# Three transformer blocks on one core: two groups of quarter products placed by a new timetable

## The chip, the cores and the metric

One core of a Trainium2 chip runs one program. The metric is device time in microseconds (us). The kernel before took 1427.65 us (median of three runs, 1426.95 to 1429.47).

## The reference

A sequence of 256 tokens of width 1024 in float32 goes through two blocks of one kind and one of another. The change concerns the first kind, and in it the two feed-forward parts:

```python
def rms_norm(x, g):
    y = xf * lax.rsqrt(jnp.mean(xf * xf, axis=-1, keepdims=True) + EPS)
    return (y * g.astype(jnp.float32)).astype(x.dtype)

def swiglu(h, w_gate_up, w_down):
    a, b = jnp.split(h @ w_gate_up, 2, axis=-1)       # 1024 -> 2 x 2816
    return (jax.nn.silu(a) * b) @ w_down              # 2816 -> 1024

def hybrid_layer(x, ...):
    x = x + 0.5 * swiglu(rms_norm(x, ffn1_norm), ffn1_w_gate_up, ffn1_w_down)
    ...                                               # pooling, attention, gates
    x = x + 0.5 * swiglu(rms_norm(x, ffn2_norm), ffn2_w_gate_up, ffn2_w_down)
    return x
```

`hybrid_layer` runs twice; a block of another kind follows, with its own feed-forward part.

## The kernel before

**Stages.** The program goes through eight stages: L0f1, L0 (mixer), L0f2, L1f1, L1, L1f2 (the four names with f are the *gated* feed-forward stages, `GATED`), then M and Mf. All 256 tokens stay in SBUF, the weights stream through.

**Precision and tiles.** A float32 product is made of three reduced ones. ACT copies each weight tile (128 x 1024, 512 KB) to a high part `whi` (line 1332), DVE subtracts to get the low part `wlo` (line 1936); such a pair of steps is called a split here. PE multiplies high by high, high by low and low by high. SP loads plain tiles into a ring of 8 buffers `raw` (line 597), waiting for the split that frees each. `whi` and `wlo` are rings of 6. ACT and DVE split some 5 and 4 tiles ahead (`ahead`).

**Gated stage.** Of the 22 blocks of 128 hidden features, two come first (group p). Twelve are *gate pairs* N2 to N10 and N15 to N17: tiles a and b, 16 matmuls of 128x512 (line 716) and 16 of 128x256 (line 723); both PSUM banks of a pair from N4 on are claimed before its first matmul. The other eight, blocks 11 to 14 and 18 to 21, are made as two *groups* (a and b in the table, chunk 0 and 1 in the code) by seven quarter products instead of eight: products 1 to 7, 12 matmuls each (lines 875 to 879). Products 3, 5, 6 and 7 use sums of the input's quarters, the input forms: DVE builds them in `xf`, ACT writes the high part `yhi` (line 1425), DVE the low part `ylo` (line 2034, `input_low`). *d i* adds block i to the output accumulators (lines 670 to 672), *T* turns a group's result for d11 and on.

**Weight forms.** Products 1 and 5 use buffer G, products 3, 7, 6 and 4 buffer H, in that order. SP loads the first form (line 615, `load_form`); each next one is made in place: when both halves of a product's tile have been split by DVE, POOL issues an accumulating DMA that adds another quarter of the weights (line 2645, `add_form`); ACT waits for it to land before it splits the next product. Group b's buffer H1 lies over `xf`, so its first load waits for the semaphore `xf_lo`, that of `input_low`. It stands in SP's queue after tile b6.

**Combining.** The products of a group are combined from PSUM by `chunk` on ACT (lines 1413 to 1421) and DVE (lines 2044 to 2060). These run when the engine comes to its next `catch_up`: after `whole(i, 0)` in a gate pair, or after the first `ahead` of a d or P step. DVE's step for product 6 releases 6's bank ("comb" + 1); ACT's SiLU of product 2 releases the bank in which 1 and 2 were summed ("sil").

**Order.** The string `ORDER` is the timetable of all five engines: PE runs it word by word, ACT and DVE do for each word their splits and what belongs to it, SP loads tiles in that order, POOL adds. `banks` hands out four PSUM banks in turn in the order of PE's claims and notes for each what frees it; banks of products 1 and 7 are held until 2 and 4 are done. So the table also sets which step each claim waits for. In the first group's last product POOL also makes tables for the next mixer (`prepare1`, `prepare2`).

```python
                        if i > 3:
                            ba, bb = claim((tag, "a", i)), claim((tag, "b", i))
                            high_part(ja, ba)
...
                    if kind == "P":
                        ahead(T[f"{tag}s{i}{n}0"])
                        catch_up()
                        ahead(T[f"{tag}s{i}{n}1"])
                        due.append((i, n))
```

Of the kernel before, what the change touches and what calls it, by code (L numbers as in the profile page):

```python
# [110 lines left out]
for _t in [f"L{l}g{j}{f}" for l in range(2) for f in range(KD) for j in range(2) if f or j]:  # L111
    HI_LEAD[_t], LO_LEAD[_t] = 4, 3
GATED = ("L0f1", "L0f2", "L1f1", "L1f2")
ORDER = """N2 N3 d0 1a N4 d1 2a N5 d2 3a N6 d3 7a N7 d4 6a N8 d5 5a N9 d6 4a N10 d7 3b d8 T0a 1b d9 T1a 7b d10 2b d11 6b
           N15 d12 5b N16 d13 4b N17 d14 d15 T0b d16 T1b d17""".split()
GROUPS = (11, 18)
CHUNK = {o + q: (c, q) for c, o in enumerate(GROUPS) for q in range(4)}
# [8 lines left out]
def steps():  # L126

    for n, word in enumerate(ORDER):
        if word[0] in "Nd":
# [7 lines left out]
def turned_hidden():  # L137

    at, out = {word: n for n, word in enumerate(ORDER)}, {}
    for i, (c, q) in CHUNK.items():  # L140
# [276 lines left out]
def build_program(nc, x_in, wstream, gains, const_in, par_in, out, cat, pat, plan, addends):  # L417
# [3 lines left out]
    with ExitStack() as ctx:  # L421
# [886 lines left out]
        def act_program(E):  # L1308
# [41 lines left out]
            def norm_hi(n, a, part=(0, 1)):  # L1350
                for g in part:
                    E.wait_ge("xt", 4 * n + 2 * a + g + 1)
                    if n:
                        E.wait_ge("tile", K.last_up(n - 1))
                    b = bank[K.BANK["xt", n, a, g][0]]
                    e.activation(feat(0, g, a), by4(b[:, :]), ACT.Copy).then_inc(sem["xhi"], 2 if n == a == 0 else 1)
# [28 lines left out]
            def gated(s):  # L1385
                tag = STAGES[s]
                f = FFNS.index(tag)
                norm_hi(s, 1)
                hi_upto(T[f"{tag}p0"] + 5)
                halves = lambda t: t.rearrange("p (n j f) -> p n j f", j=2, f=P)  # L1390
                for a in range(2):
                    E.wait_ge("tok", K.TOK[f"{tag}p"]) if a == 0 else E.wait_ge("tile", K.TOKTILE[f"{tag}p"])
                    b = bank[K.BANK[f"{tag}p", a][0]]
                    tb = tokbuf[:, a * 512:a * 512 + 512]
                    e.activation(v3d(tb[:, 0:S], 2, P), halves(b[:, :])[:, :, 0, :], ACT.Silu).then_inc(sem["tok_a"], 1)

                def low(i, part):

                    E.wait_ge("tile", DONE[f"{tag}{'ab'[part]}{i}"])
                    m = K.MUL0[s] + NORMAL.index(i)  # L1400
                    if m >= 2:
                        E.wait_ge(*(K.PROD_FREE if part else K.SIL_FREE)[m - 2])
                    e.activation((prod if part else sil)[m % 2][:, :], bank[K.BANK[tag, "ab"[part], i][0]][:, S:2 * S], ACT.Copy).then_inc(sem["low"], 1)

                def chunk(c, n):

                    cc = K.chunk_no(tag, c)
                    if n in (1, 2, 3):
                        E.wait_ge("tile", DONE[f"{tag}s{c}{n}1"])
                        b = bank[K.BANK[tag, "s", c, {2: 1}.get(n, n)][0]]  # L1410
                    if n == 1:
                        E.wait_ge("tokm", 3 * cc)
                        e.activation(tokU, b[:, :], ACT.Copy).then_inc(sem["tokp"], 1)
                    if n == 2:
                        E.wait_ge("turn", 2 * cc)
                        e.activation(tokS, b[:, :], ACT.Silu).then_inc(sem["sil"], 1)
                    if n == 3:
                        e.activation(tokV, b[:, :], ACT.Copy).then_inc(sem["tokv"], 1)
                    if n == 4:
                        E.wait_ge("comb", 5 * cc + 5)  # L1420
                        e.activation(tokU, tokU, ACT.Silu).then_inc(sem["sil"], 1)

                def input_forms():
                    E.wait_ge("xf", 6 * GATED.index(tag) + 6)
                    e.activation(yhi[:, :], xf, ACT.Copy).then_inc(sem["xf_hi"], 1)

                def turned(i):
                    c, q = CHUNK[i]
                    E.wait_ge("turn", 2 * K.chunk_no(tag, c) + q // 2 + 1)
                    if q % 2:  # L1430
                        E.wait_ge("hidlo", K.HID0[s] + i)
                    hidden_hi(K.HID0[s] + i, bank[K.BANK[tag, "turn", c, q // 2][0]][:, q % 2 * S:q % 2 * S + S])

                due = []

                def catch_up():
                    while due:
                        chunk(*due.pop(0))

                for at, kind, i, n in steps():  # L1440
                    if kind == "N":
                        ja, jb = T[f"{tag}a{i}"], T[f"{tag}b{i}"]
                        ahead(ja)
                        if i == 2:
                            E.wait_ge("ft", K.FT[tag, 0])
                            t = bank[K.BANK[tag, "ft", 0][0]]
                            for n in range(2):
                                if n:
                                    E.wait_ge("hidlo", K.HID0[s] + 1)
                                hidden_hi(K.HID0[s] + n, t[:, n * S:n * S + S])  # L1450
                        low(i, 0)
                        catch_up()
                        ahead(jb)
                        m = K.MUL0[s] + NORMAL.index(i)
                        sl = sil[m % 2][:, :]
                        E.wait_ge("sum", K.SUMV[s, i] + 1)
                        e.activation(sl, sl, ACT.Silu).then_inc(sem["act"], 1)
                        low(i, 1)
                        if i == 3:
                            input_forms()  # L1460
                        E.wait_ge("mul", K.MULV[s, i])
                        hidden_hi(K.HID0[s] + i, prod[m % 2][:, :])
                    if kind == "d":
                        ahead(T[f"{tag}d{i}"])
# [6 lines that stand above are left out]
                    for h_ in TURNED.get(at, ()):  # L1471
                        catch_up()
                        if h_ == NF - 1:
                            hi_upto(T[f"{tag}d{h_}"])
                        turned(h_)
                finish(s)
# [450 lines left out]
        def dve_program(E):  # L1927
# [70 lines left out]
            def gated(s):  # L1998
# [69 lines left out]
                for at, kind, i, n in steps():  # L2068
                    if kind == "N":
                        ja, jb = T[f"{tag}a{i}"], T[f"{tag}b{i}"]  # L2070
                        ahead(ja)
                        if i == 2:
                            t = bank[K.BANK[tag, "ft", 0][0]]
                            for n in range(2):
                                hidden_lo(K.HID0[s] + n, t[:, n * S:n * S + S])
                        whole(i, 0)
                        catch_up()
                        ahead(jb)
                        whole(i, 1)
                        m = NORMAL.index(i)  # L2080
                        pr, sl = prod_of(s, m), sil[(K.MUL0[s] + m) % 2]
                        E.wait_ge("act", K.MULV[s, i])
                        E.wait_ge("sum", K.SUMV[s, i] + 2)
                        e.tensor_tensor(pr[:, :], sl[:, :], pr[:, :], ALU.mult).then_inc(sem["mul"], 1)  # L2084
                        hidden_lo(K.HID0[s] + i, pr[:, :])
                        if i == 2:
                            input_sum(0)
                            input_sum(1)
                            input_forms()
                        if i == 3:  # L2090
                            input_low()
                    if kind == "d":
                        ahead(T[f"{tag}d{i}"])
# [6 lines that stand above are left out]
                    for h_ in TURNED.get(at, ()):  # L2100
                        catch_up()
                        if h_ == NF - 1:
                            lo_upto(T[f"{tag}d{h_}"])
                        c, q = CHUNK[h_]
                        hidden_lo(K.HID0[s] + h_, bank[K.BANK[tag, "turn", c, q // 2][0]][:, q % 2 * S:q % 2 * S + S])
# [853 lines left out]
```

## Time and profile before

| | |
|---|---|
| median of three runs | 1427.65 us |
| the profiled execution | 1427.81 us |
| its span | 1426.0 us |
| PE matmul | busy 1414.3 us, 99% |
| DVE | busy 1063.6 us, 75% |
| ACT | busy 838.7 us, 59% |
| POOL | busy 200.9 us, 14% |
| DMA | 292.90 MB, mean 205 GB/s |
| TensorE clock | full in all 40 slices |

The profile is of one execution; its times count from the start of the span. An engine's waits are listed by what released it. A busy share says little here: PE is the engine that sets the time, and what others do matters where PE waits for it. Matmuls are pipelined: one of 128x512 is shown with 0.39 us, and the next starts 0.23 us after it.

### The profile page before, as it was taken

The numbers are of one execution on the slowest core, as the hardware profiler recorded it, in microseconds if no ns is written. First come the engines' busy times: TensorE is split into PE (matmuls) and PEld (weight loads), VectorE is DVE, ScalarE is ACT, GpSimd is POOL, SyncE is SP. The second block draws the span as 40 slices with busy tenths as digits, with TensorE's granted clock in tenths as the row PEclk, the third lists the DMA queues.
The fourth block names the chain that finished last, engine by engine and source line by source line (L and its number), as shares of the span: only waits on it lengthen the run. The fifth ranks groups of instructions, "written<-read, shape, count | busy, mean of one in ns | idle before, by whom it ended". The sixth has DMA issues, their size and how long they took to land.

```text
span 1426.0 us, 20401 instructions
## 1 busy us (share of the span) xinstructions
PE 1414.3 (99%) x7776; PEld 1207.5 (85%) x7776; DVE 1063.6 (75%) x1638; ACT 838.7 (59%) x1397; POOL 200.9 (14%) x275
## 2 busy tenths in 40 slices
PE   9999999999999999999999999999999999999999
PEld 7888888898888888888888898888888899888887
DVE  7777776676867778786776678777776867778776
ACT  6556556755665556664566746655557765455553
POOL 0121023000001000210050000141048300100000
PEclk9999999999999999999999999999999999999999
DMA  9979665456887768967564466969646335456551
GB/s 376 310 215 241 202 214 180 134 192 226 264 233 182 213 235 271 251 171 213 192 236 148 163 216 184 306 188 244 198 160 222 134 121 192 161 166 219 194 189 59
DMA packets 80592, 292.90 MB, mean 205 GB/s; under 512 B 8944, under 2 KB 9072, under 8 KB 80368
## 3 DMA queue, kind: packets, MB, share of 16 engines
q1 hardware_dynamic: 70992, 257.26, 51.5%
q0 software_dynamic: 9216, 33.56, 13.0%
q8 instruction: 62, 1.02, 0.3%
q10 hardware_dynamic: 288, 0.79, 0.1%
q14 instruction: 34, 0.28, 0.1%
HBM read 290.52 MB, written 1.05 MB: 204 GB/s over the span
## 4 chain that ended last, share of the span: by engine, by line
PE 92%; DVE 5%; ACT 1%; DMA 1%; issue 0%; SPq 0%; DVEq 0%; ACTq 0%
PE bank L716 19%; PE bank L723 10%; PE bank L670 8%; PE bank L671 8%; PE bank L672 8%; PE bank L737 4%; PE bank L742 4%; PE bank L738 4%; PE bank L875 3%; PE bank L879 3%; PE bank L876 3%; PE bank L700 3%; PE bank L707 3%; PE bank L701 3%; DVE wlo L1936 2%; PE bank L969 1%
## 5 line engine op out<-in xcount | busy, mean ns | idle before, releaser
L1936 DVE TENSOR_TENSOR wlo<-raw,whi 128x1024 fp32r<-128x1024 f32 (+1 forms) x433 | 523.4, 1235 | 12.7 <-ACT whi L1332 12.7
L1332 ACT ACTIVATE whi<-raw 128x1024 fp32r<-128x1024 f32 (+1 forms) x433 | 443.0, 1049 | 6.0 <-DMA raw<-w_dram 2.9
L716 PE MATMUL bank<-hx,whi 128*128 128x512 f32 x1344 | 330.8, 393 | 2.1 <-issue 2.1
L716 PEld LDWEIGHTS bank<-hx,whi 128*128 128x128 f32 x1344 | 247.6, 188 | 54.7 <-issue 6.3
L670 PE MATMUL bank<-whi,hid 128*128 128x512 f32 x536 | 211.8, 395 | 0.0
L671 PE MATMUL bank<-wlo,hid 128*128 128x512 f32 x536 | 209.6, 391 | 0.0
L672 PE MATMUL bank<-whi,hid 128*128 128x512 f32 x536 | 208.8, 390 | 0.0
L723 PEld LDWEIGHTS bank<-hx,wlo 128*128 128x128 f32 x1344 | 176.0, 191 | 13.4 <-DVE wlo L1936 4.5
L723 PE MATMUL bank<-hx,wlo 128*128 128x256 f32 x1344 | 179.5, 283 | 3.7 <-DVE wlo L1936 3.7
L1361 ACT ACTIVATE hid<-prod 128x256 fp32r<-128x256 f32 x94 | 39.3, 418 | 161.0 <-DVE prod L2084 75.9
L672 PEld LDWEIGHTS bank<-whi,hid 128*128 128x128 f32 x536 | 100.6, 188 | 21.7
L670 PEld LDWEIGHTS bank<-whi,hid 128*128 128x128 f32 x536 | 101.0, 188 | 18.8 <-issue 0.7
L671 PEld LDWEIGHTS bank<-wlo,hid 128*128 128x128 f32 x536 | 101.0, 188 | 17.2
L737 PE MATMUL bank<-whi,hx 128*128 128x512 f32 (+1 forms) x256 | 101.9, 399 | 1.2 <-DVE hx L1964 0.9
L738 PE MATMUL bank<-whi,hx 128*128 128x512 f32 (+1 forms) x256 | 98.1, 384 | 0.0
L742 PE MATMUL bank<-wlo,hx 128*128 128x512 f32 (+1 forms) x256 | 77.5, 385 | 0.0
L1969 DVE TENSOR_TENSOR hid<-prod,hid 128x256 fp32r<-128x256 f32 x94 | 40.0, 426 | 47.0 <-ACT hid L1361 47.0
L2600 POOL TENSOR_SCALAR small<-small 128x1 f32<-128x1 f32 x15 | 10.7, 713 | 451.4 <-ACT arena L1347 451.4
L1936 DVE TENSOR_TENSOR wlo<-gates,whi 128x1024 fp32r<-128x1024 f32 x48 | 57.6, 1225 | 20.7 <-ACT whi L1332 20.7
L1936 DVE TENSOR_TENSOR wlo<-arena,whi 128x1024 fp32r<-128x1024 f32 x48 | 57.2, 1219 | 12.5 <-ACT whi L1332 12.5
L1332 ACT ACTIVATE whi<-arena 128x1024 fp32r<-128x1024 f32 x48 | 48.9, 1050 | 29.0 <-DMA arena<-w_dram 29.0
L1332 ACT ACTIVATE whi<-gates 128x1024 fp32r<-128x1024 f32 x48 | 49.4, 1053 | 26.0 <-DMA gates<-w_dram 26.0
(300 smaller groups left out, 2188.2 us busy)
## 6 DMA issues: line engine op xcount, KB each, us to landing
raw<-w_dram SPq DMA_DIRECT2D x438, 512.0 KB, 4.4
gates<-w_dram POOLq DMA_DIRECT2D x32, 512.0 KB, 6.7
arena<-w_dram POOLq DMA_DIRECT2D x32, 512.0 KB, 7.6
gates<-w_dram SPq DMA_DIRECT2D x16, 512.0 KB, 6.6
arena<-w_dram SPq DMA_DIRECT2D x16, 512.0 KB, 6.5
gain<-g_dram SPq DMA_DIRECT2D x7, 512.0 KB, 3.4
arena<-c_dram SPq DMA_DIRECT2D x2, 768.0 KB, 6.4
cst<-c_dram SPq DMA_DIRECT2D x1, 1056.0 KB, 10.2
```

The source lines that it names most:

```text
L670: e.matmul(psum, shi, mhi, start=first, stop=False, skip_group_check=True)
L671: e.matmul(psum, shi, mlo, start=False, stop=False, skip_group_check=True)
L672: return e.matmul(psum, slo, mhi, start=False, stop=last, skip_group_check=True)
L700: e.matmul(psum, whj[:, w:w + P], hi(k), start=k == 0, stop=False, skip_group_check=True)
L701: e.matmul(psum, whj[:, w:w + P], lo(k), start=False, stop=False, skip_group_check=True)
L716: e.matmul(b[:, :], hi_of(j)[:, k * P:k * P + P], hx[:, k * 2 * S:k * 2 * S + 2 * S], start=k == 0, stop=False, skip_group_check=True)
L723: ins = e.matmul(b[:, 0:S], lo_of(j)[:, k * P:k * P + P], hiT(k), start=False, stop=k == KD - 1, skip_group_check=True)
L737: e.matmul(b[:, 0:n], hiT(k, a * P, a * P + P), w, start=k == 0, stop=False, skip_group_check=True)
L738: e.matmul(b[:, 0:n], loT(k, a * P, a * P + P), w, start=False, stop=False, skip_group_check=True)
L742: ins = e.matmul(b[:, 0:n], hiT(k, a * P, a * P + P), w, start=False, stop=k == KD - 1, skip_group_check=True)
L1332: e.activation(hi_of(t), raw_of(t), ACT.Copy).then_inc(sem["w_hi"], 1)
L1936: e.tensor_tensor(lo_of(t), raw_of(t), hi_of(t).bitcast(F32), ALU.subtract).then_inc(sem["w_lo"], 1)
```

## The change

The low part of the input forms is made on DVE after gate pair N4 instead of N3. The timetable has another order from d4 on up to N15: product 5a before N8, then the rest of group a and products 3b, 1b, 7b and 2b each earlier against the gate pairs; d10 and d11 stand next to each other before 6b. ACT's copy of product 3 waits in the second group for the first multiply of the group before.

```diff
-ORDER = """N2 N3 d0 1a N4 d1 2a N5 d2 3a N6 d3 7a N7 d4 6a N8 d5 5a N9 d6 4a N10 d7 3b d8 T0a 1b d9 T1a 7b d10 2b d11 6b
+ORDER = """N2 N3 d0 1a N4 d1 2a N5 d2 3a N6 d3 7a N7 d4 6a 5a N8 d5 4a N9 d6 3b N10 d7 1b d8 T0a 7b d9 T1a 2b d10 d11 6b
            N15 d12 5b N16 d13 4b N17 d14 d15 T0b d16 T1b d17""".split()
...
                     if n == 3:
+                        if cc:
+                            E.wait_ge("tokm", 3 * cc - 2)
                         e.activation(tokV, b[:, :], ACT.Copy).then_inc(sem["tokv"], 1)
...
-                        if i == 3:
+                        if i == 4:
                             input_low()
```

In the order of the changed program the lines from 1418 on have numbers larger by 2.

**DVE, gate pairs N3 and N4 of stage L0f1.** hid3 belongs to N3, hid0 to N4; `wlo` from `raw` are splits of plain tiles. Before:

```order
L1969 TENSOR_TENSOR hid3<-prod1,hid3 128x256 [waits s_hidhi]
L2034 TENSOR_TENSOR ylo<-arena,yhi 128x2048 [waits s_xf_hi]
L1936 TENSOR_TENSOR wlo<-raw,whi 128x1024 [waits s_w_hi] x4
L2014 TENSOR_TENSOR sil0<-sil0,bank0 128x256 [waits s_low]
L1936 TENSOR_TENSOR wlo<-raw,whi 128x1024 [waits s_w_hi]
L2014 TENSOR_TENSOR prod0<-prod0,bank1 128x256 [waits s_low]
```

Now:

```order
L1971 TENSOR_TENSOR hid3<-prod1,hid3 128x256 [waits s_hidhi]
L1938 TENSOR_TENSOR wlo<-raw,whi 128x1024 [waits s_w_hi] x4
L2016 TENSOR_TENSOR sil0<-sil0,bank0 128x256 [waits s_low]
L1938 TENSOR_TENSOR wlo<-raw,whi 128x1024 [waits s_w_hi]
L2016 TENSOR_TENSOR prod0<-prod0,bank1 128x256 [waits s_low]
L2086 TENSOR_TENSOR prod0<-sil0,prod0 128x256 [waits s_sum,s_act,s_hidlo]
L1971 TENSOR_TENSOR hid0<-prod0,hid0 128x256 [waits s_hidhi]
L2036 TENSOR_TENSOR ylo<-arena,yhi 128x2048 [waits s_xf_hi]
```

`ylo` moved behind four splits, one more, and N4's own steps.

**SP, from the second group's first load of G on, stage L0f1** (the same in both programs): the first two `arena` rows are form G of group b, the row that waits for `xf_lo` is form H of group b.

```order
L615 DMA arena<-w_dram 128x1024 [waits s_sq_v,s_sq]
L615 DMA arena<-w_dram 128x1024
L597 DMA raw<-w_dram 128x1024 [waits s_w_lo]
L615 DMA arena<-w_dram 128x1024 [waits s_xf_lo]
L615 DMA arena<-w_dram 128x1024
L597 DMA raw<-w_dram 128x1024 [waits s_w_lo] x2
L622 DMA cst<-c_dram 128x2112
```

Nothing moved here; what moved is the DVE step that `xf_lo` stands for.

**DVE, from the end of N7 to N8, stage L0f1.** hid3 is N7's; `wlo` from `gates` are splits of form tiles; line 2044 (2046 now) is the step for product 6. Before:

```order
L1969 TENSOR_TENSOR hid3<-prod1,hid3 128x256 [waits s_hidhi]
L1936 TENSOR_TENSOR wlo<-raw,whi 128x1024 [waits s_w_hi] x2
L1936 TENSOR_TENSOR wlo<-gates,whi 128x1024 [waits s_w_hi] x2
L2014 TENSOR_TENSOR sil0<-sil0,bank1 128x256 [waits s_low]
L2044 TENSOR_TENSOR arena<-arena,bank2 128x512 [waits s_tokp,s_tile]
```

Now:

```order
L1971 TENSOR_TENSOR hid3<-prod1,hid3 128x256 [waits s_hidhi]
L1938 TENSOR_TENSOR wlo<-gates,whi 128x1024 [waits s_w_hi]
L1938 TENSOR_TENSOR wlo<-raw,whi 128x1024 [waits s_w_hi] x3
L2046 TENSOR_TENSOR arena<-arena,bank2 128x512 [waits s_tokp,s_tile]
L1938 TENSOR_TENSOR wlo<-gates,whi 128x1024 [waits s_w_hi] x2
```

The step for product 6 comes before N8's `whole` now, and behind four splits as before. On **PE**, product 5a (lines 875 to 879) began behind d5 (lines 670 to 672), a gate pair after 6a:

```order
L671 MATMUL bank7<-wlo,hid1 128x512
L672 MATMUL bank7<-whi,hid1 128x512
L875 MATMUL bank2<-whi,yhi 128x512 [waits s_w_hi,s_comb]
L876 MATMUL bank2<-whi,ylo 128x512
L875 MATMUL bank2<-whi,yhi 128x512
```

Now 5a stands in front of N8 (line 716):

```order
L879 MATMUL bank1<-wlo,yhi 128x512 [waits s_w_lo]
L879 MATMUL bank1<-wlo,yhi 128x512
L716 MATMUL bank3<-hx,whi 128x512 [waits s_w_hi,s_comb,s_sum]
L716 MATMUL bank3<-hx,whi 128x512 x7
L716 MATMUL bank2<-hx,whi 128x512 [waits s_w_hi]
```

The wait for "comb", the release of product 6's bank, was 5a's and is N8's now.

## Rows read from the trace of the kernel before

**Rows 1.** Waits of PE, the whole span: us in total, times, longest us.

```profile
PE bank L723 <- DVE wlo L1936: 3.7, 4, 0.9
PE bank L716 <- issue: 2.1, 3, 1.0
```

**Rows 2.** Timeline of PE, N4 and d1 of L0f1: start, length.

```profile
43.15 1.11 PE L723 MATMUL bank<-hx,wlo 128*128 128x256 f32 x8
45.17 1.22 PE L723 MATMUL bank<-hx,wlo 128*128 128x256 f32 x8 [0.91 <-DVE wlo L1936]
46.40 0.47 PE L670 MATMUL bank<-whi,hid 128*128 128x512 f32 x1
```

**Rows 3.** Chain that ended last: N8 of three stages, N15 of L1f1.

```profile
85.10 3.63 PE bank L716 x16
88.72 1.91 PE bank L723 x16
...
417.48 3.63 PE bank L716 x16
...
655.11 1.05 issue
656.15 3.88 PE bank L716 x16
...
933.08 3.63 PE bank L716 x16
```

**Rows 4.** Timeline of DVE, N3's end to product 3a's splits, L0f1.

```profile
41.70 2.29 DVE L2034 TENSOR_TENSOR ylo<-arena,yhi 128x2048 fp32r<-128x2048 f32 x1
43.90 4.63 DVE L1936 TENSOR_TENSOR wlo<-raw,whi 128x1024 fp32r<-128x1024 f32 x4
...
51.37 0.43 DVE L1969 TENSOR_TENSOR hid<-prod,hid 128x256 fp32r<-128x256 f32 x1 [0.48 <-ACT hid L1361]
...
53.98 2.35 DVE L1936 TENSOR_TENSOR wlo<-gates,whi 128x1024 fp32r<-128x1024 f32 x2
```

**Rows 5.** Timeline of ACT before N15, stage L1f1.

```profile
651.40 1.06 ACT L1332 ACTIVATE whi<-arena 128x1024 fp32r<-128x1024 f32 x1 [3.86 <-DMA arena<-w_dram]
...
655.47 0.58 ACT L1416 ACTIVATE arena<-bank 128x512 f32<-128x512 f32 x1
```

**Rows 6.** Timeline of SP's queue, L0f1: form H of group b, next tiles.

```profile
45.52 0.91 SPq L615 DMA_DIRECT2D arena<-w_dram  x2
46.47 1.27 SPq L597 DMA_DIRECT2D raw<-w_dram  x2
```

**Rows 7.** DMA rate in 40 slices of 1.5 us from 15 to 75 us.

```profile
GB/s 412 410 404 415 410 404 407 412 412 404 412 412 391 243 134 16 44 150 249 423 415 421 268 355 377 442 420 415 412 345 270 270 284 270 284 410 421 380 259 262
```

**Rows 8.** Timeline of ACT, L0f1: split of 6a's second tile, low of N7.

```profile
80.43 1.06 ACT L1332 ACTIVATE whi<-gates 128x1024 fp32r<-128x1024 f32 x1 [2.81 <-DMA gates<-w_dram]
...
82.34 0.36 ACT L1403 ACTIVATE sil<-bank 128x256 f32<-128x256 f32 x1
```

**Rows 9.** Timeline of DVE, L0f1: splits behind N7, step for product 6.

```profile
86.08 2.54 DVE L1936 TENSOR_TENSOR wlo<-raw,whi 128x1024 fp32r<-128x1024 f32 x2
...
90.93 0.41 DVE L2014 TENSOR_TENSOR sil<-sil,bank 128x256 f32<-128x256 f32 x1
91.26 0.67 DVE L2044 TENSOR_TENSOR arena<-arena,bank 128x512 f32<-128x512 f32 x1
```

**Rows 10.** The same splits of ACT in L0f2 and L1f2.

```profile
407.35 1.07 ACT L1332 ACTIVATE whi<-gates 128x1024 fp32r<-128x1024 f32 x1 [0.26 <-DMA gates<-w_dram]
...
411.09 0.38 ACT L1403 ACTIVATE sil<-bank 128x256 f32<-128x256 f32 x1 [1.73 <-PE bank L723]
...
924.31 1.07 ACT L1332 ACTIVATE whi<-gates 128x1024 fp32r<-128x1024 f32 x1 [0.40 <-DMA gates<-w_dram]
```

**Rows 11.** Timeline of DVE, L0f2: splits behind N7.

```profile
414.84 2.35 DVE L1936 TENSOR_TENSOR wlo<-raw,whi 128x1024 fp32r<-128x1024 f32 x2
```

**Rows 12.** Timeline of DVE, L1f1: the split in N7.

```profile
593.62 3.17 DVE L1936 TENSOR_TENSOR wlo<-raw,whi 128x1024 fp32r<-128x1024 f32 x1
```

## What the change does to the time, predicted

> **What bounds the kernel now.** I read the page first: TensorE is busy for 1414.3 of 1426.0 us, so only its waits can be won or added. The waits by engine [rows 1] name two kinds inside the four gated feed-forward stages: four waits for a `wlo` piece of DVE (3.7 us) and three put down to "issue" (2.1 us).
>
> *Wait A*, once in each stage, is in [rows 2]. The low part of N4's second tile (line 723) starts 2.02 us after the first instead of 0.96 (half of the 1.91 that the chain shows for N8 in [rows 3]); the next step starts 1.23 us later instead of 0.96; with a slow first matmul of 0.07 that is 1.4 us. [Rows 4] show why on DVE: the low part of the input forms (`ylo`, 2.29 us) runs at 41.70, ahead of four `wlo` splits that only begin at 43.90; the first is what PE waits for at 45.17, the second holds d1.
>
> *Wait B* is at N15, and only in the three later stages. In stage L1f1 the chain [rows 3] shows 1.05 us of "issue" before it, and a group of 16 that takes 3.88 us where N8's takes 3.63. On ACT [rows 5] a split waited 3.86 us for the added form of product 6b to land, and the SiLU of product 2b (line 1416), whose bank N15 claims, came behind it and ended at 656.05, just before PE starts at 656.15. Three such waits: 2.1 us of [rows 1], and some 0.3 each of slow restart, 3.0 in all.
>
> **The sum, part by part.** The profiled execution took 1427.81 us for a span of 1426.0; the median shown is 1427.65, 0.16 less. To set stages side by side I subtract 332.38 and 847.98 us from times of L0f2 and L1f2: the differences of their N8 starts to 85.10 [rows 3].
>
> 1. *`input_low` one gate pair later.* The four `wlo` splits run at about 41.7 to 46.4, the two that PE wants ending near 42.9 and 44.1 instead of 45.1 and 46.3 (1.14 us apiece). Wait A goes: 4 x 1.4 = -5.6 us. The hidden low of N4 (51.37) comes 2.2 us sooner, `ylo` behind it at about 49.5 to 51.8, and the splits of [rows 4] that follow, the first product-3 split ending at 55.1, keep their times: `ylo` only changed sides. No product needs `ylo` before 3a at about 59.
>
> 2. *What is queued behind `ylo`.* SP waits for it (`xf_lo`) before it loads form H of the second group, and SP is one queue. Today these loads leave at 45.52 and the raw tiles behind them at 46.47 [rows 6], waiting for splits alone. Now SP holds from about 43 to 51.8: two form loads and all raw tiles behind are issued some 6 us late, in one burst of eight, in the stretch in which POOL's accumulating loads of product 3's form (issued after the split of 55.1) want the same 16 DMA engines. The rate [rows 7] shows that they are full when work is there (412 to 423 GB/s, 1.3 us for 512 KB) and were nearly empty from 38 to 42: the new pause is not made up. The raw tiles themselves have room; the chain 3a, add, 7a, add, 6a does not.
>
> 3. *5a ahead of N8.* PE's work is the same, but N8 now claims the bank that product 6a filled, and this is free after DVE's `chunk` 6 (line 2044, 0.68 us). On DVE that step now stands behind four splits after the hidden low of N7, where it used to be wanted only by 5a, a gate pair later. Let L be the time at which the second added form of 6 has landed and ACT splits it. In L0f1 L is 80.43 [rows 8]; low of N7 follows at 82.34, the hidden low ends and the splits start at 86.08, four splits take until 90.93 (4.85), then chunk 6 0.68 [rows 9]: 91.6, L + 11.2. N8 would start at 85.10 + 2.72 (12 matmuls of 5a at 3.63/16 us) - 1.4 = 86.4. So **PE waits 5.2 us in L0f1**, even if L stays. None of this work is new; its cover, the gate pair between it and its user, is gone.
>
> 4. *The other three stages.* In L0f2 L is 407.35 - 332.38 = 75.0 and low of N7 then waited 1.73 us for PE [rows 10]: bound by PE, the splits begin 3.75 us after that low part (414.84) [rows 11], so chunk 6 ends at 78.7 - 1.4 + 3.75 + 4 x 1.14 + 0.68 = 86.3: no wait. But L itself moves by part 2. Its ends: 75.0 as today, and 80.4 as in L0f1, where two more loads of constants (1.9 MB, 4.7 us of full DMA) lie in the same stretch as the delayed burst will now in all stages. I take 78.0, a little on L0f1's side, since the pause of part 2 costs about as much DMA time as those loads. Chunk 6 then ends at 78.0 + 11.2 less 0.3 (splits not slowed) = 88.9 in L0f2: wait 2.5. L1f2, whose L today is 924.31 - 847.98 = 76.3 [rows 10], gets the slowed splits and 0.3 more: 3.1. L1f1: one split took 3.17 us instead of 1.22 while POOL made its tables [rows 12], and these now lie before the critical step: between 0 and 1.95 more, I take 1.0: 3.8. Sum of the new waits 5.2 + 2.5 + 3.1 + 3.8 = +14.6 us.
>
> The row of 3.17 us bears on a rule of the Trainium skill, page "SBUF — State Buffer", section "Who interferes with whom": a DVE instruction with two SBUF inputs and a GpSimd one that reads SBUF exclude each other for a whole instruction. By it every split that meets a table instruction can lose up to that instruction's length, also in L0f1 and L1f2; the measured splits there lost 0.05 to 0.1 each, so the sum goes by the rows.
>
> 5. *New timetable after d6.* 3b moves ahead of N10 and 7b ahead of T1a, so that product 7b's add leaves a step earlier, and two accumulations stand between 2b and 6b. The split of 6b that waited 3.86 us is then met by data that landed some 5 us before; the SiLU of 2b ends several us ahead of N15. Wait B goes: -3.0. Bounds: -3.0 to 0.
>
> 6. *The added wait* of ACT's copy of product 3b for the first multiply of the group before: that multiply stands a gate pair ahead of it in DVE's order. Nothing. POOL and SP issue the same DMAs, none added; POOL's move with their splits.
>
> Sum: -5.6 - 3.0 + 14.6 = +6.0 us, 1433.8 in the profiled execution's terms, **1433.6** for a median.
>
> **Rivals.** *L stays as today in the three later stages* (the adds have a share of the engines that a raw backlog can't take). Then L0f1 waits 5.2, L1f2 (L 76.3, chunk 6 at 87.5) 1.1, L1f1 0 to 2: -8.6 + 6.3 to 8.3, or 1425.4 to 1427.4. For it: the bytes are the same, only later. Against: the 5.4 us by which L0f1's L is later [rows 8, 10], with nothing different there but more plain loads.
>
> *The other side: the held SP queue clears the way for POOL's adds.* If the first add gets going before the burst fills the engines, it lands some 3 us earlier even in L0f1, and the chain gains that at each link. Once L is below about 75.2 in every stage chunk 6 ends at 86.3 by PE's own pace, the waits at N8 vanish, and -8.6 is left: 1419.2. Against: SP issues from 51.8, the add at 55.5, so the burst is there first.
>
> *Wait B stays* (the new bank order makes N15 wait for another step as long): +3.0 on the forecast, 1436.6.
>
> *The clock falls.* Every stretch of this profile has TensorE at its full granted clock, 2.4 GHz, with no wait of PE above 1.0 us inside a stage [rows 1]. A wait of 4 to 5 us in L0f1 is new. If the level dropped to 1.2 GHz behind it, the work of one gate pair and one accumulation (8.3 us at full rate) would be bounded by 8.3 us more, I take 5: 1438.6. The Trainium skill, "TensorE: Matmul & The Clock Gate", section "Why this matters for your kernels", speaks against such gaps, since idle time takes the clock back to half; no run shown here has a gap that long.
>
> *It doesn't do what it says*: `ylo` may be moved and wait A be kept, if the splits wait for ACT instead; but the four ran back to back behind `ylo` (4.63 us) with no wait for ACT [rows 4], so I give this no chance of its own.
>
> **How the numbers follow.** What can be told from no change is 0.2%, 2.9 us. Forecast (waits at N8 in all stages, 1430 to 1440): 0.60. L as today: 0.18. Adds freed: 0.08. B stays: 0.07. Clock: 0.07. Faster by over 0.2% (below 1424.8): 0.08 and a part of the second case, 0.12; within 0.2%: 0.18; slower: 0.70. The range must take in L as today (1426 and above) and L = 80.4 in every stage (waits of 5.2, 4.9, 5.2 and 5.2 to 7, near 1440); it leaves out the freed adds and the worst of the clock: 1426 to 1440.
>
> **What would show it.** Right: no wait for `wlo` at N4; SP's form load of the second group at about 52 us; ACT's splits of 6a at 78 to 80 in the later stages; a PE wait at N8 (line 716) for DVE's line 2046, 5 us in L0f1 and 2 to 4 in the others; nothing at N15. Wrong: L at 75 or below after the burst, chunk 6 done before 86.4, or PE waits at places that I have not named (T0a, 4a), which would mean that the bank order was read wrongly.

## The result, and the profile after

The changed kernel takes **1455.38 us** (median of four runs, 1452.95 to 1457.24) against 1428.34 us for the kernel before, measured beside it: 1.0189 times as long, 95% interval 1.017 to 1.0207. The forecast was 1433.6 us, the range 1426 to 1440. The profiled execution took 1457.24 us for a span of 1455.4 us, so the two profiles stand 29.4 us apart and the medians 27.0 (the profiled execution was the slowest of the four).

The waits of PE in the changed kernel, whole span (us in total, times, longest), answer to [rows 1]:

```profile
PE bank L716 <- issue: 13.9, 4, 3.6
PE bank L879 <- DVE wlo L1938: 5.0, 4, 1.4
PE bank L737 <- ACT arena L1891: 2.7, 1, 2.7
```

Both old kinds are gone: nothing waits for a split at N4, nothing at N15. Three new kinds have come: four waits at N8, four inside product 5a, one in the mixer M. PE's timeline around N8 of L0f1 (start, length, idle before):

```profile
88.92 0.73 PE L879 MATMUL bank<-wlo,yhi 128*128 128x512 f32 x2 [1.41 <-DVE wlo L1938]
93.21 5.80 PE L716 MATMUL bank<-hx,whi 128*128 128x512 f32 x16 [3.55 <-issue]
98.84 2.08 PE L723 MATMUL bank<-hx,wlo 128*128 128x256 f32 x16
```

N8's sixteen matmuls take 5.80 us, where N8 took 3.63 us in [rows 3]. The same view has 5.51 us for it in L0f2 and 6.26 us in L1f1. The reason is in the windows of the changed kernel, the mean granted clock standing third from the end:

```profile
88.00:98.00 10.00, 5.52 (x15) 4.12 (x16) 7.38 (x7) 5.01 (x6) 5.11 (x6) 0.66 0.83 246
426.00:436.00 10.00, 5.45 (x17) 4.04 (x17) 7.46 (x8) 5.28 (x6) 0.00 (x0) 0.83 0.65 194
612.00:622.00 10.00, 5.49 (x15) 3.79 (x14) 7.99 (x8) 5.61 (x6) 5.72 (x7) 0.70 0.71 200
952.00:962.00 10.00, 5.10 (x14) 3.49 (x13) 8.29 (x8) 5.90 (x7) 10.00 (x19) 0.77 0.67 200
1131.00:1141.00 10.00, 7.33 (x32) 6.10 (x31) 9.05 (x17) 5.50 (x13) 9.37 (x10) 0.70 0.46 157
```

TensorE left its full level, 2.4 GHz, for the lower one, 1.2 GHz, in all four stages and once in M, each time at a wait of PE. On DVE the rows that answer to [rows 9] and [rows 4] are these (L0f1):

```profile
41.35 4.62 DVE L1938 TENSOR_TENSOR wlo<-raw,whi 128x1024 fp32r<-128x1024 f32 x4
...
49.16 2.28 DVE L2036 TENSOR_TENSOR ylo<-arena,yhi 128x2048 fp32r<-128x2048 f32 x1
...
87.25 0.42 DVE L1971 TENSOR_TENSOR hid<-prod,hid 128x256 fp32r<-128x256 f32 x1 [0.48 <-ACT hid L1361]
87.59 1.27 DVE L1938 TENSOR_TENSOR wlo<-gates,whi 128x1024 fp32r<-128x1024 f32 x1
88.79 3.72 DVE L1938 TENSOR_TENSOR wlo<-raw,whi 128x1024 fp32r<-128x1024 f32 x3
92.44 0.67 DVE L2046 TENSOR_TENSOR arena<-arena,bank 128x512 f32<-128x512 f32 x1
```

The splits for N4 now come 2.2 us sooner, ahead of `ylo`. Behind N7's hidden low part stand four splits and only then the step for product 6, done at 93.11; N8 starts at 93.21. The split at 87.59 is that of 5a's second tile, and 5a waits for it. SP's queue in the same stage, which answers to [rows 6]:

```profile
42.60 0.33 SPq L597 DMA_DIRECT2D raw<-w_dram  x1
51.47 0.80 SPq L615 DMA_DIRECT2D arena<-w_dram  x2
52.32 0.91 SPq L597 DMA_DIRECT2D raw<-w_dram  x2
```

ACT's splits of 6a's second tile in L0f1, L0f2 and L1f2 answer to [rows 8, 10]:

```profile
81.95 2.01 ACT L1332 ACTIVATE whi<-gates 128x1024 fp32r<-128x1024 f32 x2 [2.49 <-DMA gates<-w_dram]
...
420.33 2.01 ACT L1332 ACTIVATE whi<-gates 128x1024 fp32r<-128x1024 f32 x2 [2.79 <-DMA gates<-w_dram]
...
946.95 2.01 ACT L1332 ACTIVATE whi<-gates 128x1024 fp32r<-128x1024 f32 x2 [2.28 <-DMA gates<-w_dram]
```

Counted from the start of N4 in each stage, the split starts at 42.8, 40.9, 40.4 (L1f1) and 42.5 us, where it started at 40.9, 35.5, 35.9 and 36.9 us before.

**The ledger.** PE does the same 7776 matmuls in both, so the time a step takes from its first matmul to that of the next can be compared stage by stage (changed minus before, us):

| | L0f1 | L0f2 | L1f1 | L1f2 | sum |
|---|---|---|---|---|---|
| N4 and d1 (wait A) | -1.4 | -1.4 | -1.4 | -1.4 | -5.7 |
| 7a and 6a | 1.5 | 0 | 0 | 1.2 | 2.8 |
| N7 and d4 | 0.1 | 0.1 | 0 | 0.2 | 0.4 |
| 5a, up to N8's first matmul | 5.6 | 5.0 | 5.0 | 5.6 | 21.1 |
| N8 itself | 2.0 | 1.7 | 2.5 | 2.9 | 9.1 |
| 6b up to N15, and N15 (wait B) | 0 | -0.5 | -1.4 | -1.2 | -3.1 |
| from the end of L1f2 to the end (M) | | | | | 5.2 |
| ahead of the first stage | | | | | -0.3 |

That is 29.5 us, against 29.4 between the profiles.

### The profile page after: what moved, and what is told of

It reads as the page before. It is cut to its first block, busy times and chain, and to the rows that moved or that the text cites. A ratio compares the mean times of both kernels' runs of the same rounds, so it can differ in the third digit from the quotient of the medians.

```text
span 1455.4 us, 20396 instructions
## 1 busy us (share of the span) xinstructions
PE 1427.1 (98%) x7776; PEld 1214.3 (83%) x7776; DVE 1062.7 (73%) x1638; ACT 839.8 (58%) x1397; POOL 206.0 (14%) x275
## 4 chain that ended last, share of the span: by engine, by line
PE 76%; DVE 10%; DMA 6%; ACT 3%; POOL 3%; issue 2%; DVEq 0%; ACTq 0%; POOLq 0%
PE bank L716 16%; PE bank L723 8%; PE bank L670 7%; PE bank L671 7%; PE bank L672 7%; DMA gates<-w_dram 6%; DVE wlo L1938 6%; PE bank L737 3%; PE bank L742 3%; PE bank L738 3%; PE bank L700 3%; PE bank L707 3%; PE bank L701 3%; PE bank L879 2%; PE bank L875 2%; PE bank L876 2%
## 5 line engine op out<-in xcount | busy, mean ns | idle before, releaser
L716 PE MATMUL bank<-hx,whi 128*128 128x512 f32 x1344 | 339.7, 401 | 13.9 <-issue 13.9
L716 PEld LDWEIGHTS bank<-hx,whi 128*128 128x128 f32 x1344 | 253.8, 193 | 69.4 <-issue 18.6
L1403 ACT ACTIVATE sil<-bank 128x256 f32<-128x256 f32 x48 | 18.1, 376 | 81.5 <-PE bank L723 81.5
L2647 POOL DMA_DIRECT2D gates<-w_dram x32 | 28.1, 879 | 255.3 <-DVE wlo L1938 255.3
```

The costliest lines, as they stand in the source:

```text
L716: e.matmul(b[:, :], hi_of(j)[:, k * P:k * P + P], hx[:, k * 2 * S:k * 2 * S + 2 * S], start=k == 0, stop=False, skip_group_check=True)
```

## The experiments

Each kernel ran beside the kernel before on the same chip; the medians of that one were 1427.5, 1428.7, 1428.8 and 1428.3 us in the four sittings. In the table, the columns 7a, 6a, 5a and N8 are sums over the four stages: by how many us these steps were longer than without a wait or slow clock. A step ends where the next begins, so a wait ahead of N8 counts in the step in front of it: 5a in the changed timetable, 6a in the old one (ylo_only). An N8 that was less than 0.2 us longer counts nothing. (In fill14 the added matmuls count in 5a; in lazy the wait lies inside N8.)

| run | 7a, 6a | 5a | N8 | wait in M | us | ratio, 95% interval |
|---|---|---|---|---|---|---|
| changed kernel | 2.8 | 21.1 | 9.1 | 2.7 | 1455.4 | 1.017 to 1.0207 |
| order_only | 0 | 6.7 | 3.2 | 2.7 | 1437.5 | 1.0042 to 1.0081 |
| ring | 2.2 | 21.4 | 7.9 | none | 1450.5 | 1.0139 to 1.0174 |
| fill14 | 2.3 | 20.3 | 0 | 2.7 | 1446.9 | 1.0109 to 1.0151 |
| h33 | 0 | 10.4 | 2.6 | 2.7 | 1437.4 | 1.0041 to 1.0074 |
| early6 | 1.6 | 7.4 | 0 | 2.7 | 1433.1 | 1.002 to 1.0042 |
| lazy | 1.7 | 7.1 | 7.7 | 2.7 | 1439.1 | 1.0053 to 1.0087 |
| h33_cst | 1.4 | 10.1 | 6.8 | 2.7 | 1441.2 | 1.0068 to 1.0104 |
| h33_cst_early | 0 | 8.1 | 0 | 2.7 | 1435.3 | 1.0026 to 1.0066 |
| allfix | 0 | 0.7 | 0 | none | 1419.7 | 0.9915 to 0.9952 |
| ylo_only | 7.3 | 0 | 0 | none | 1431.0 | 1.0016 to 1.0038 |
| ylo_h31 | 0 | 0 | 0 | none | 1422.3 | 0.9935 to 0.9969 |
| b_only | 0 | 0 | 0 | none | 1424.2 | 0.9951 to 0.9977 |
| best1 | 0 | 0 | 0 | none | 1419.0 | 0.991 to 0.9943 |

**The low input forms alone (ylo_only).**

```diff
-                        if i == 3:
+                        if i == 4:
                             input_low()
```

> The kernel before with one edit: the low part of the input forms is made after gate pair N4 instead of N3; the timetable is the old one. Theory (the held SP queue makes product 6's second added form late, and only the new timetable lacks the cover for that): wait A goes in four stages, 1.4 us each, and product 6a's second tile is split some 5 us later in the three later stages than before, but still ahead of its use: 1428.3 - 5.6 = 1422.7 us, no wait above 1 us in a gated stage but those at N15. Rival 1 (holding SP costs PE time by itself, whatever the timetable): waits at 7a, 6a or 5a of 1 to 3 us a stage, 1427 to 1433 us. Rival 2 (the adds are not delayed by it): 1422.7 us as well, but product 6a's split in the later stages at its old distance from N2 (about 53 us behind N2 instead of 58).

1431.0 us: rival 1. Wait A went in all four stages, but PE waits at N8 in each (and once in 7a). PE's waits in this kernel:

```profile
PE bank L716 <- DVE prod L2014: 4.2, 4, 1.2
PE bank L716 <- issue: 2.7, 3, 1.0
```

Line 2014 is `whole`, which frees a bank of N7. It stands on DVE behind the split of 6a's second tile, and that split starts 40.7 to 43.3 us behind N4's start instead of 35.5 to 40.9. So a late product 6 reaches N8 in the old timetable too, through another bank. The second line is wait B, longer now (2.7 us in all, 2.1 before).

**The timetable alone (order_only):** the changed kernel with `input_low` back at 3.

> The changed kernel with the low part of the input forms back after N3: the new timetable alone. Theory (held SP queue makes product 6 late): in L0f1 the split of 6a's second tile is late with or without it, so a wait at N8 of about 3.5 us and some slow clock stays there; in the three later stages product 6's step is done 5 us sooner than in the changed kernel and the waits at 5a and N8 shrink to 0 to 1.5 us with the clock at full rate. Wait A is back (+5.6), wait B gone (-2.7), mixer M as in the changed kernel (+5.1): 1436 to 1442 us. Rival (the new timetable makes product 6 late by itself, by the adds' own order or by DVE's queue): the stall in each stage is only shorter by the 1.4 us that PE loses at wait A, 1453 to 1457 us.

1437.5 us, as the theory said. The split of 6a's second tile is back at 34.8 to 36.4 us in the later stages, and the excess at 5a is 4.0, 0.1, 2.0 and 0.6 us by stage. One stage came out worse than the theory had it: in L1f1 PE waited 1.87 us at N8 and the clock fell behind it. In L0f1 the split stands where it stood before (40.9), so the 4.0 us there are the price of the order alone.

**Form H of the second group loaded after tile a8 (h33).**

```diff
-                            at = T[f"{tag}p0"] + {"G": (6, 20), "H": (8, 22)}[buf][c]
+                            at = T[f"{tag}p0"] + {"G": (6, 20), "H": (8, 33)}[buf][c]
```

> The changed kernel, but the load of form H of the second group stands in SP's queue after tile a8 instead of after tile b6. There `xf_lo` has long been set, so SP is not held and the raw tiles leave when their buffers come free. Theory (the held queue and its burst make product 6's second added form late): that form lands as in the run with the new timetable alone, and each stage's excess at 5a is that run's (4.0, 0.1, 2.0, 0.6 us) plus the 1.4 us that PE is earlier without wait A, some 12 us in all instead of 21; half clock in one or two stages instead of four, 3 to 4 us instead of 9; the 2.7 us at 7a and 6a go. With M as in the changed kernel: 1438 to 1441 us. Rival (it is `ylo`'s new place on DVE that makes the splits of 3a, 7a and 6a late, not SP): nothing but a us or two of change, 1453 to 1456 us.

1437.4 us: the theory, a little below its range. SP no longer stands still, and the split starts 37.2 to 39.7 us behind N4's start instead of 40.4 to 42.8. The adds show how the held queue did it: in L0f2 the two that make product 6's form (line 2647, issued near 408.2 and 412.0 us in the changed kernel) took 8.2 and 8.3 us from issue to landing there, and 5.6 and 5.4 us in h33. In the 11 us from the first of these adds on, the DMA engines moved 3.54 MB in the changed kernel and 2.50 MB in h33: the burst was still going on. SP's queue in L0f1:

```profile
42.78 2.60 SPq L597 DMA_DIRECT2D raw<-w_dram  x3
...
46.38 6.75 SPq L597 DMA_DIRECT2D raw<-w_dram  x3
53.17 0.91 SPq L615 DMA_DIRECT2D arena<-w_dram  x2
```

The same repair in the old timetable (**ylo_h31**, form H after a8 there too):

> The kernel before with the low input forms after N4 and form H of the second group loaded after tile a8; the timetable is the old one. Theory (the 9 us by which the low forms moved alone missed their gain come from SP being held): the split of 6a's second tile ends 37 to 38 us behind N4's start in the later stages instead of 40.7 to 41.5, the waits at 7a and at N8 go, wait A is gone, wait B stays (2.7): 1428 - 5.6 = 1422.4 us. Rival (the splits' new order on DVE costs it): 1428 to 1431 us.

1422.3 us: wait A is gained whole once SP is not held. The 9 us between ylo_only and this run are the price of the held queue (7.3 us of it ahead of N8 and in 7a, some 2 at wait B); `ylo`'s new place on DVE costs nothing by itself.

**DVE's step for product 6 ahead of three splits (early6).**

```diff
                     if kind == "P":
+                        if (i, n) == (0, 6):
+                            chunk(i, n)
                         ahead(T[f"{tag}s{i}{n}0"])
                         catch_up()
                         ahead(T[f"{tag}s{i}{n}1"])
-                        due.append((i, n))
+                        if (i, n) != (0, 6):
+                            due.append((i, n))
```

> The changed kernel, but DVE's step for product 6 of the first group (line 2046) is run at the head of product 6's own splits, ahead of three splits of plain tiles, instead of behind them. Every engine's work is the same. Theory (N8's second bank waits for that step, which stands behind splits that nobody wants yet): the step ends near 89.5 us in L0f1 instead of 93.1, N8 starts right behind 5a, no wait at N8 in any stage and the clock stays full; only 5a's own wait for a split stays, 1.0 to 1.4 us a stage (excess 1.9 instead of 5.0 to 5.6, and nothing of the 9.2 us of slow N8): 1455.4 - 4 x 3.5 - 9.2 = 1432 us. Rival 1 (5a's wait of 1.4 us alone takes the clock down): 1438 to 1441 us. Rival 2 (splits that come behind the step are late for N8 and d5 in their turn): waits of the same size at lines 716 or 670, 1445 us or more.

1433.1 us, again the theory. DVE and PE in L0f1:

```profile
88.82 0.67 DVE L2046 TENSOR_TENSOR arena<-arena,bank 128x512 f32<-128x512 f32 x1
89.42 3.67 DVE L1938 TENSOR_TENSOR wlo<-raw,whi 128x1024 fp32r<-128x1024 f32 x3
```

```profile
88.95 0.73 PE L879 MATMUL bank<-wlo,yhi 128*128 128x512 f32 x2 [1.40 <-DVE wlo L1938]
```

The splits are the same, but the step is done 3.6 us sooner, and N8 follows 5a at once; 5a's wait of 1.4 us stays, and the clock stays full in the four stages. Claiming N8's second bank late does part of it (**lazy**):

```diff
-                            ba, bb = claim((tag, "a", i)), claim((tag, "b", i))
+                            ba = claim((tag, "a", i))
                             high_part(ja, ba)
+                            bb = claim((tag, "b", i))
```

> The changed kernel, but a gate pair claims its second bank behind the eight matmuls of its first tile's high part (1.8 us) instead of ahead of them. Theory (N8 waits for its second bank alone, that of product 6): those 1.8 us run during the wait, which falls from 3.5 to 1.7 us in each stage, and the clock falls in fewer stages or none: between 1455.4 - 7.2 = 1448 us with the clock as it is and 1439 us with the clock full in the gated stages; I take 1441 us. Rival (N8's first bank or tile is late too): 1453 us or more.

1439.1 us. PE in L0f1 shows that N8's first bank was free all the time:

```profile
88.95 2.00 PE L716 MATMUL bank<-hx,whi 128*128 128x512 f32 x8
92.63 2.11 PE L716 MATMUL bank<-hx,whi 128*128 128x512 f32 x8 [1.68 <-DVE arena L2047]
```

**The clock by itself (fill14).** 14 matmuls between 5a and N8's second claim, into a bank that N8 overwrites.

> The changed kernel with 14 matmuls of 128x512 (3.2 us at the full clock) more, issued between product 5a and N8 into the bank of N8's first tile, which that tile's own first matmul overwrites; N8's second bank is claimed after them. They fill most of the 3.3 to 3.6 us for which PE waits there and change no output. Theory (TensorE falls to half its clock because it stands still there): N8 runs at the full clock and the 1.7 to 3.0 us by which it was slow in each stage go, 9.2 us in all: 1446 us, or a little more where the wait in 5a (1 to 1.4 us) is enough by itself. Rival (the clock falls for another reason, such as the load of the chip, or the slow stretch follows the wait in 5a): 1455 us or more, with the half clock still there.

1446.9 us. N8 starts no earlier (93.24), but runs in 3.92 us, and the window of the same ten microseconds as above has a granted clock of 1.00:

```profile
93.24 3.92 PE L716 MATMUL bank<-hx,whi 128*128 128x512 f32 x16 [0.34 <-DVE arena L2051]
```

```profile
88.00:98.00 10.00, 8.66 (x41) 7.04 (x42) 7.55 (x7) 5.10 (x6) 5.19 (x6) 1.00 0.84 246
```

So standing still costs the wait and then 1.7 to 2.9 us more, and work that nobody needs wins that part back: 8.5 us by the medians.

**The banks in another rotation (ring):** `deque([3, 1, 0, 2])` for `deque([0, 1, 2, 3])` in `banks`.

> The changed kernel with the four PSUM banks handed out from the start in the order 3, 1, 0, 2 instead of 0, 1, 2, 3. Nothing else differs: the same waits in the gated stages, only other bank numbers, so that mixer M meets the banks as in the kernel before. Theory (the new timetable leaves the ring of banks in another rotation, and in M the product Mmo claims the bank that ACT empties last, line 1891): the wait of 2.7 us in M and the slow clock behind it go, 5.1 us in all: 1450.3 us. Rival (the stall in M is a disturbance of that one execution, or comes from transfers that are later): no change, 1455.4 us.

1450.5 us, to 0.2 us what the theory said. The table sets more than the gated stages: it hands the four banks on in another order. The claim of product Mmo in M, in the order of PE's instructions, before and in the changed kernel:

```
L737 MATMUL bank<-whi,hx 128x512 [waits s_w_hi,s_mqk_ev]
L737 MATMUL bank<-whi,hx 128x512 [waits s_w_hi,s_mv_ev]
```

`mv_ev` is ACT's copy of the product just made (line 1891). PE and ACT there, changed kernel:

```profile
1131.22 1.86 PE L1194 MATMUL bank<-arena 128*128 128x30 f32 x16
1135.76 0.79 PE L737 MATMUL bank<-whi,hx 128*128 128x512 f32 x1 [2.67 <-ACT arena L1891]
```

```profile
1132.77 1.99 ACT L1332 ACTIVATE whi<-raw 128x1024 fp32r<-128x1024 f32 x2
1134.66 1.05 ACT L1891 ACTIVATE arena<-bank 128x512 f32<-128x512 f32 x2
```

**The constants of L0f1 (h33_cst, h33_cst_early):** h33 with the two loads of constants behind tile b8, and behind tile d2.

> The changed kernel with form H of the second group loaded after tile a8 and, in the first stage, the two loads of constants (1.9 MB) after tile b8 instead of eight tiles sooner. It differs from the run with the form load alone in stage L0f1 only. Theory (the constants take the DMA engines while product 3's and 7's forms are added, which is why product 6's form is 2 us later in L0f1 than in the later stages): L0f1's split of 6a's second tile ends 37.5 us behind the start of N4 instead of 39.7, the excess at 5a falls from 4.25 to about 2 us and N8 runs at the full clock (2.66 less): 1437.4 - 4.5 = 1433 us. Rival (L0f1 is late for another reason, such as fewer transfers in flight at the start): no change, 1437 us.

1441.2 us, a miss: L0f1 got worse. There SP issues the constants at 54.6, just ahead of the adds that turn product 3's form into product 7's, and ACT's splits of product 7's form come 2.3 and 3.1 us later behind N4's start than in h33, hence the 1.4 us at 7a. The three other stages have the same edit as h33 and much the same waits, of about 2 us (1.5 to 2.5 in h33), but here the clock fell behind each. The mean clocks of its four executions, 0.992 to 0.995, do not make the profiled one an exception.

> The changed kernel with form H of the second group loaded after tile a8 and, in the first stage, the two loads of constants after tile d2: SP issues them near 28 us, and their 1.9 MB fall into the stretch from 35 to 42 us in which the DMA engines stood nearly still. It differs from the run with the form load alone in stage L0f1 only. Theory (the constants hold up what is issued behind them, and product 6's form is late in L0f1 by their time): there the second add for product 7's form lands some 5.5 us after its issue, as in the later stages, instead of 8.7; the split of 6a's second tile ends 38 to 39 us behind N4's start instead of 40.8, the wait at N8 falls from 3.5 to about 1.5 us and N8 runs at the full clock: 1437.4 - 4.5 = 1433 us. Rival (the plain tiles' own backlog at the start of the program makes it late): 40.8 us and 1437 us as before.

The theory holds for its mechanism: ACT's split in L0f1, h33 and then this run:

```profile
79.10 2.01 ACT L1332 ACTIVATE whi<-gates 128x1024 fp32r<-128x1024 f32 x2 [2.76 <-DMA gates<-w_dram]
```

```profile
76.94 2.01 ACT L1332 ACTIVATE whi<-gates 128x1024 fp32r<-128x1024 f32 x2 [1.05 <-DMA gates<-w_dram]
```

From N4's start 39.7 and 37.4 us, and L0f1's excess at 5a is 2.0, like the others'. The median came down by 2 us where 4.5 were expected. By the mean clocks it fell in some executions and not in others: the profiled execution took 1431.6 us at a mean clock of 0.999, the slowest of the six 1437.4 us at 0.995.

**The second group's part of the timetable alone (b_only).**

```diff
- ... N9 d6 4a N10 d7 3b d8 T0a 1b d9 T1a 7b d10 2b d11 6b
+ ... N9 d6 4a 3b N10 d7 1b d8 T0a 7b d9 T1a 2b d10 d11 6b
```

> The kernel before with the second group's part of the new timetable alone (product 3b ahead of N10, 1b ahead of d8, 7b ahead of T1a, 2b ahead of d10) and ACT's added wait; 5a stays behind d5 and the low input forms behind N3. Theory: wait B goes (0.4, 1.3 and 1.1 us in the three later stages), nothing else moves, the banks come to M in their old rotation: 1427.5 - 2.7 = 1424.8 us. Rival (the products of the second group, each closer to the one before, wait for their added forms or banks, which the changed kernel does not show because its first group is late): new waits in 3b, 1b or 7b, 1428 us or more.

1424.2 us, 4.5 below the kernel before beside it; by the steps of the profiles it is 3.1, wait B as a whole. This part is a plain gain; PE waits nowhere in the gated stages but at wait A.

**Everything repaired, in either timetable (allfix, best1).** allfix is the changed kernel with early6, h33 and ring; best1 is the kernel before with b_only's table, `input_low` at 4 and form H after a8.

> The changed kernel with three repairs at once: DVE's step for product 6 of the first group at the head of 6's splits, form H of the second group loaded after tile a8, and the banks handed out from 3, 1, 0, 2. The timetable is the changed one. Theory (each stall of the changed kernel has one of these causes, and they add up): no wait at N8, none in M, full clock throughout; at 5a the wait for its second tile's low split stays, since that split stands behind N7's hidden low part (1.9 us in L0f1, 1.6 to 1.9 in the others): 1428 - 5.6 - 2.7 + 7 = 1427 us. Rival 1 (5a's wait was due to the late added form and goes as well): 1420 us. Rival 2 (a repair uncovers a new wait, at d5 or 4a): above 1430 us.

> The kernel before with three edits: the second group's part of the new timetable with ACT's added wait, the low input forms after N4, and the load of form H of the second group after tile a8 in SP's queue, so that SP is not held. Theory: waits A and B both go and the waits at 7a, 6a and N8 that the earlier low forms brought with the old SP order (1.6 to 3.4 us a stage) stay away, but for L0f1, where product 6's form is late by two loads of constants: 1427.5 - 5.6 - 2.7 + 1 to 2 = 1420 to 1421 us. Rival 1 (the low input forms are late for other reasons than SP): as with the low forms moved alone, 1427 to 1429 us. Rival 2 (without wait A, PE meets the adds at 7a and 6a earlier in every stage): 1 us a stage, 1423 us.

1419.7 and 1419.0 us, the same within what can be told, and both 0.7% faster than the kernel before. In allfix rival 1 was right: 5a's wait too had been due to the late form, since DVE reaches that split only behind 6a's. The window of best1's first gated stage has PE busy in all of it:

```profile
22.40:178.80 156.40, 156.40 (x790) 133.03 (x788) 121.44 (x151) 95.59 (x140) 21.90 (x29) 1.00 0.83 257
```

## Why the prediction was wrong

The direction was right, the size was not: +6 us forecast, +27 measured, 15 us above the range. Three things of the prediction failed. Step 4 took the time L of product 6's form 3 us later than before where it came 5 us later, and step 2 gave the held queue no price at 7a and 6a: 9.3 us together, enough by themselves to leave the range. The clock behind the forecast waits stood in the sum with nothing: 9.1 us. And the bank order was not followed past the gated stages, to mixer M: 5.2 us. By the prediction's own steps:

1. *Wait A*, -5.6 us: measured -5.7.
2. *What is queued behind `ylo`*: SP held until about 51.8, measured 51.5. h33 and ylo_h31 show that this hold makes product 6's form late. But the step gave it no price of its own. 7a and 6a cost 2.8 us, and ylo_only shows 7.3 us, with the waits at N8, even in the old timetable, where the prediction saw cover.
3. *5a ahead of N8*: the step for product 6 ends at "L + 11.2"; with L = 81.95 it ended at 93.11. early6 shows that its place behind the splits is what N8 waits for, and order_only that the order alone costs L0f1 4.0 us (5.2 less the 1.4 of wait A would be 3.8). The forecast of 5.2 us for L0f1 stands against 5.6; that 1.4 of it lies inside 5a was not seen, and costs nothing more. L itself, taken as unchanged in L0f1 (80.43), came 1.5 us later, but PE too was 1.5 us late by then, from 7a and 6a, so the wait hardly grew.
4. *The other three stages*: this is the mis-sized term. L was taken 3.0 us later in L0f2 than before, "a little on L0f1's side"; it came 5.4 us later there, 4.6 in L1f1, 5.6 in L1f2. The upper bound, L0f1's lateness in every stage, was the truth. Waits of 2.5, 3.8 and 3.1 us (L0f2, L1f1, L1f2) became 5.0, 5.0 and 5.6: the 14.6 us are 21.1. The 1.0 us for POOL's tables in L1f1 did not come: the four splits and the step for product 6 took there what they took in L0f1 (612.20 to 617.72 and 87.59 to 93.11, 5.5 us both), so two errors of opposite sign stood in the 3.8. That constants make L0f1's form late was right, as h33_cst_early shows; that the burst weighs as much as they do was a guess, and too low. Why L1f2 is later than L0f2 and L1f1, 42.5 against 40.9 and 40.4 us from N4's start, no run shows.
5. *Wait B*, -3.0: measured -3.1, and b_only shows it alone.
6. *ACT's added wait*, nothing: nothing.

The larger error lies outside the steps. *The clock* was a rival of 0.07, priced at 5 us in one stage; it fell in four, at 1.7 to 2.9 us each, and in M. fill14 shows 8.5 us for the four. A forecast with four waits of 2.5 to 5.2 us should have carried a price for it, not left it to a rival. The Trainium skill, "TensorE: Matmul & The Clock Gate", section "Why this matters for your kernels", warns that idle gaps take the engine back to half its clock; the trace agrees, with N8's 5.80 us for 3.63. *Mixer M* was in no step: 5.2 us from the rotation of the banks, shown by ring. The prediction read what the table does to claims in the gated stages, and did not follow the same allocator into the stage behind them.

In sum: 6.0 forecast, + 6.5 (steps 3 and 4), + 2.8 (step 2), + 9.1 (clock), + 5.2 (M) = 29.6 us, against 29.4 between the profiles. Of the rivals, "L as today", "adds freed" and "B stays" were all wrong.

The row of 3.17 us [rows 12] had been weighed against the page "SBUF — State Buffer" of the Trainium skill, section "Who interferes with whom", by which a DVE instruction with two SBUF inputs and a GpSimd instruction that reads SBUF exclude each other. The splits lost little here again (1.24 us apiece where POOL made tables, 1.16 in L0f2 where it did not). It is POOL that lost here: see below.

## What to carry to other kernels

Moving a step out of an engine's way moves everything that waits for its semaphore: look first at in-order queues of loads, where one held transfer holds all behind it. Where a table or an allocator sets which resource each step claims, follow it to the end of the program, not only to the end of the stage that was edited. And where a forecast holds a wait of several microseconds on TensorE, add what the clock can take behind it, here 1.7 to 2.9 us a time.

## What was not expected of the hardware

*The clock does not follow the length of the wait alone.* In h33, N8 of L0f2, L1f1 and L1f2 started behind waits of 1.67, 2.54 and 1.47 us and ran at the full clock. In h33_cst three waits of 1.94 to 2.07 us all took it down, and one of 1.87 us did in order_only. All waits of 3.3 us or more did, and M's of 2.7 us too. PE's timeline at N8 of L1f1, h33 and then h33_cst:

```profile
608.44 3.91 PE L716 MATMUL bank<-hx,whi 128*128 128x512 f32 x16 [2.54 <-issue]
```

```profile
609.79 5.49 PE L716 MATMUL bank<-hx,whi 128*128 128x512 f32 x16 [1.96 <-issue]
```

In h33_cst_early waits of 1.64 to 2.25 us left it at full. What decides between them is open; it also makes such a kernel's times scatter, 1431.6 to 1437.4 us for one program.

*DVE and POOL slow each other, and which one pays varies.* POOL's small table instructions in the changed kernel's L0f1, the same operation in front of DVE's row of splits and beside it:

```profile
87.12 0.25 POOL L2614 TENSOR_TENSOR arena<-cst,par 128x32 f32<-128x32 f32 x1
...
89.01 1.23 POOL L2614 TENSOR_TENSOR arena<-cst,par 128x32 f32<-128x32 f32 x1
```

Five times as long, while the splits lost 0.08 us each. Spans on POOL are rough in such a record, but the whole row fits: the four that run beside the splits (87.75 to 92.68) take 1.23 to 1.30 us, and the two behind them, beside DVE's step for product 6, which reads one side from PSUM, take 0.25 us again. The row of 3.17 us [rows 12] is the other case: in the kernel before, L1f1, POOL's table row began at 593.00 and DVE's split behind it at 593.62:

```profile
593.00 0.63 POOL L2668 TENSOR_SCALAR small<-par 128x16 f32<-128x16 f32 x1
593.25 0.66 POOL L2611 TENSOR_TENSOR arena<-cst,par 128x64 f32<-128x64 f32 x1
...
595.17 0.52 POOL L2613 TENSOR_TENSOR arena<-cst,par 128x32 f32<-128x32 f32 x1
```

POOL went on there at one instruction in 0.2 to 0.3 us, and the split was the one to lose, 2 us. What decides who loses stays open: POOL's row had begun ahead of DVE's splits in both stretches.
